# Twelve blocks scaled and shifted on ScalarE in place of VectorE, and modulation units placed earlier, in a two-block transformer kernel

## What is computed

```python
mod = silu(c) @ w_ada + b_ada                  # c: 2048; w_ada: 2048 x 12288
sh1, sc1, gt1, sh2, sc2, gt2 = split(mod, 6)
h = rms_norm(x, g_pre_mix) * (1.0 + sc1) + sh1
proj = h @ w_in                                # conv, attention, index and gate inputs
...
mixed = (g_conv * y_conv + g_attn * y_attn) @ w_o
x = x + gt1 * rms_norm(mixed, g_post_mix)
h = rms_norm(x, g_pre_ffn) * (1.0 + sc2) + sh2
f = (silu(h @ w_gate) * (h @ w_up)) @ w_down
x = x + gt2 * rms_norm(f, g_post_ffn)
```

## Time and profile before

| | us |
|---|---|
| median of 3 runs (2555.86 to 2557.14) | 2556.08 |
| the profiled execution | 2557.15 |
| its span, first to last instruction | 2555.3 |
| TensorE busy, matmuls | 2519.6 |
| VectorE busy | 1857.3 |
| ScalarE busy | 1269.6 |

### The profile page before, as it was taken

The page is one execution under the profiler, slowest core; times in us unless marked ns, Lnnn a source line. Parts: engine busy times, 40 slices in busy tenths (PEclk is TensorE's granted clock), DMA queues, the critical chain, the costliest instruction groups (busy, mean ns, idle before and its releaser), DMA issues.

```text
span 2555.3 us, 30126 instructions
## 1 busy us (share of the span) xinstructions
PE 2519.6 (99%) x11400; PEld 2072.9 (81%) x11400; DVE 1857.3 (73%) x2333; ACT 1269.6 (50%) x1733; POOL 3.9 (0%) x11
## 2 busy tenths in 40 slices
PE   7999999999999999999999999999999999999998
PEld 5888878888878888888888787888888888888886
DVE  7999999998877677556765667666666674456665
ACT  4445777764564444444444545554554444444443
POOL 0000000000000000000000000000000000000000
PEclk9999999999999999999999999999999999999999
DMA  9998666888946656665555555445555555555553
GB/s 378 355 355 318 216 214 217 294 296 313 361 168 229 231 210 238 243 231 210 217 215 198 185 194 180 162 170 197 181 193 188 196 208 198 189 195 198 187 194 130
DMA packets 80643, 578.23 MB, mean 226 GB/s; under 512 B 9022, under 2 KB 9318, under 8 KB 10737
## 3 DMA queue, kind: packets, MB, share of 16 engines
q1 hardware_dynamic: 78768, 566.92, 60.9%
q10 hardware_dynamic: 1218, 6.70, 0.7%
q0 software_dynamic: 512, 2.69, 0.3%
HBM read 574.15 MB, written 3.70 MB: 226 GB/s over the span
## 4 chain that ended last, share of the span: by engine, by line
PE 90%; DVE 5%; issue 1%; ACT 1%; DMA 0%; DVEq 0%; ACTq 0%; SPq 0%
PE bank L750 86%; DVE wlo L1643 2%; DVE raw L1653 1%; DVE cv L1854 1%; PE bank L689 1%; DMA raw<-in_w_in 0%; ACT whi L1075 0%; PE bank L905 0%; PE bank L953 0%; ACT PR L1075 0%; DVE PART L1716 0%; PE bank L867 0%; PE bank L996 0%; DVE SC L1798 0%; PE bank L1016 0%
## 5 line engine op out<-in xcount | busy, mean ns | idle before, releaser
L1643 DVE TENSOR_TENSOR wlo<-raw,whi 128x1024 fp32r<-128x1024 f32 x882 | 1072.9, 1223 | 632.8 <-ACT whi L1075 630.2
L1075 ACT ACTIVATE whi<-raw 128x1024 fp32r<-128x1024 f32 x882 | 929.5, 1058 | 1090.6 <-PE bank L750 942.6
L750 PE MATMUL bank<-whi,HTh 128*128 128x512 f32 x2560 | 697.7, 394 | 9.1 <-ACT HTh L1075 5.8
L750 PE MATMUL bank<-wlo,HTh 128*128 128x512 f32 x2560 | 687.0, 390 | 2.4 <-DVE wlo L1643 2.4
L750 PE MATMUL bank<-whi,HTl 128*128 128x512 f32 x2560 | 687.4, 390 | 0.0
L750 PEld LDWEIGHTS bank<-wlo,HTh 128*128 128x128 f32 x2560 | 480.9, 188 | 104.6 <-DVE wlo L1643 3.9
L750 PEld LDWEIGHTS bank<-whi,HTh 128*128 128x128 f32 x2560 | 473.9, 188 | 110.6 <-issue 10.8
L750 PEld LDWEIGHTS bank<-whi,HTl 128*128 128x128 f32 x2560 | 481.2, 188 | 101.4
L1653 DVE CUSTOM_DVE_ANT_0 raw<-raw,GT,VECS 128x2048 f32<-128x2048 f32 x96 | 224.8, 2346 | 0.4 <-DMA raw<-in_w_ada 0.2
L750 PE MATMUL bank<-whi,ACTl 128*128 128x512 f32 x704 | 188.8, 389 | 0.0
L750 PE MATMUL bank<-whi,ACTh 128*128 128x512 f32 x704 | 188.8, 389 | 0.0
(11 more groups left out here) (242 smaller groups left out, 1173.0 us busy)
## 6 DMA issues: line engine op xcount, KB each, us to landing
raw<-in_w_in SPq DMA_DIRECT2D x128, 1024.0 KB, 5.0
raw<-in_w_ada SPq DMA_DIRECT2D x96, 1024.0 KB, 6.1
raw<-in_w_gate SPq DMA_DIRECT2D x88, 1024.0 KB, 4.8
raw<-in_w_up SPq DMA_DIRECT2D x88, 1024.0 KB, 4.8
raw<-in_w_down SPq DMA_DIRECT2D x88, 1024.0 KB, 4.8
raw<-in_w_o SPq DMA_DIRECT2D x16, 1024.0 KB, 7.3
raw<-in_w_out SPq DMA_DIRECT2D x16, 1024.0 KB, 4.8
raw<-in_w_attn_out SPq DMA_DIRECT2D x8, 1024.0 KB, 5.0
```

Of the source, the lines that this page charges most:

```text
L750: i = e.matmul(bank[2 * ch.st + t][:, :], (xl if ps == 1 else xh)[:, k, tk(t)], (lo if ps == 2 else hi)[:, j * 512:j * 512 + 512], start=c ...
L1075: return e.activation(dst, src, ACT.Copy, scale=scale)
L1643: e.tensor_tensor(lo, src, r32(hi), S_).then_inc(lo_done, 1)
```

## The change

On VectorE, groups 2, 3 and 4 of `first_h` lose their scale-and-shift operations. ScalarE makes them, all of a group before its copies, as an activation with MA as scale and MB as bias, in place on xT, and waits for the group's MA first. VectorE's subtraction waits for both. In the plan, the condition for a modulation unit in the first stage becomes another one, and the share of the output projection 0.57 in place of 0.70.

```diff
--- before.py
+++ after.py
@@ -140,7 +140,7 @@
             else:
                 ch = p.chunk("part", (j, n), "h", "ACT" if j == 0 else "DVE", st=3 if n % 2 else 1)
             p.mm(ch, "w_in", (c * 4 + j) * 128 * 2048, 4, 512, 4 * j)
-            p.ada(early if j < 3 else p.later, int(n < (8 if j else 9)))
+            p.ada(early or p.later, int(n < (8, 8, 9, 10)[j] or (j, n) == (0, 8)))
     p.here("kiwi")
     p.ada(p.later, 1)
     p.mm(p.chunk("kiwi", 0, "h", "ACT", evictions=1), "w_kiwi", 0, 16, 80, 0)
@@ -165,7 +165,7 @@
         p.cols(p.chunk("conv", j, "ct", "DVE"), "w_conv_out", j, range(2), 2, 0.5)
     p.here("wo")
     for j in range(4):
-        p.cols(p.chunk("wo", j, "mix", "DVE", apart=j == 3), "w_o", j, range(4), 4, 0.7)
+        p.cols(p.chunk("wo", j, "mix", "DVE", apart=j == 3), "w_o", j, range(4), 4, 0.57)
     assert not p.later
     p.later += [(5, c) for c in range(16)]
     plan_ffn(p, 0, "")
@@ -417,7 +417,8 @@
     pro_pe = steps("pro_pe", list(R(4)))
     xt_pe = steps("xt_pe", list(R(0, 16, 2)))
     xt_act = steps("xt_act", list(R(0, 16, 2)))
-    fh_dve = steps("fh_dve", [(k, c) for cs_ in HG for k in ("h", "lo") for c in cs_])
+    fh_dve = steps("fh_dve", [(k, c) for cs_ in HG for k in (("h", "lo") if cs_[0] < 4 else ("lo",)) for c in cs_])
+    h_act = steps("h_act", list(R(4, 16)))
     fh_act = steps("fh_act", list(R(16)))
     rb_pe = steps("rb_pe", ["rows"])
     rb_act = steps("rb_act", ["rows"])
@@ -1198,8 +1199,15 @@
             yield 1
 
         def first_h(g):
+            if g > 1:
+                w.wait_ge(*first_mod(g))
+                w.wait_ge(*ada_of(0, HG[g][-1]))
+                for c in HG[g]:
+                    w.wait_ge(*xt_act(c // 2 * 2))
+                    e.activation(xT[:, c, :], xT[:, c, :], ACT.Identity, bias=MB[:, 0, c:c + 1],
+                                 scale=MA[:, 0, c:c + 1]).then_inc(*h_act.one(c))
             for c in HG[g]:
-                w.wait_ge(*fh_dve("h", c))
+                w.wait_ge(*(h_act(c) if g > 1 else fh_dve("h", c)))
                 copy(HTh[:, c, :], xT[:, c, :]).then_inc(*fh_act.one(c))
             yield 1
 
@@ -1675,13 +1683,13 @@
             stt(js, js, 1.0, vec("g1", HG[g][0], len(HG[g])), A_, M_).then_inc(*first_mod.one(g))
             w.wait_ge(*first_mod(g))
             w.wait_ge(*ada_of(0, HG[g][-1]))
-            for c in HG[g]:
+            for c in HG[g] if g < 2 else ():
                 w.wait_ge(*xt_act(c // 2 * 2))
                 e.tensor_scalar(xT[:, c, :], xT[:, c, :], MA[:, 0, c:c + 1], MB[:, 0, c:c + 1], M_, A_).then_inc(
                     *fh_dve.one("h", c))
             for c in HG[g]:
                 w.wait_ge(*fh_act(c))
-                w.wait_ge(*fh_dve("h", c))
+                w.wait_ge(*(fh_dve("h", c) if g < 2 else h_act(c)))
                 e.tensor_tensor(HTl[:, c, :], xT[:, c, :], r32(HTh[:, c, :]), S_).then_inc(*fh_dve.one("lo", c))
             yield 1
```

## The result

The changed kernel takes 2566.94 us (median of 5 runs, 2564.85 to 2568.35), the kernel before 2556.21 us beside it (5 runs, 2555.86 to 2557.14). The ratio is 1.0039 with a 95% interval of 1.0028 to 1.0050: **10.7 us slower**, between 7 and 13. Forecast were 6.0 us. The sign was right, the size was not, and the median lies 1.1 us above the range. The profiled execution took 2568.35 us with a span of 2566.5, so the two traces differ by 11.2 us.

A forecast was written before the change was run, and what follows sets the result against it. TensorE bounds the kernel generally, but VectorE is slower in the changed stage, by 0.30 us per 1 MB weight unit. 1.5 + 1.1 + 2.27 + 1.1 gives 6.0 us, so the median 2556.08 becomes 2562.1 us; range 2557.7 to 2565.8.

The forecast's parts named there:

- The three groups: Groups 2, 3, 4 of `first_h`: VectorE waits for ScalarE's scale-and-shift and gets 1.5, 1.1 and 1.1 us later.
- The unit at 58: Extra modulation unit at piece 58, where VectorE is the slower engine: costs 2.27 us.
- TensorE inherits it all: At the `qiT` copy near 214 us, TensorE takes over VectorE's whole delay, 6.0 us, whatever its cover before.
- Rival B: Delay partly hidden: ScalarE is quick and only the unit at piece 58 counts, 2.27 us, 2558.4; chance 0.14.
- rival C: Stalls at 202 and 218 us lower TensorE's granted clock: 2563.8 for one fall, 2565.5 for two; chance 0.12.
- the two units at 78 and 80: Extra modulation units before kiwi: 4.54 us more of VectorE, hidden by its waits and lead, so cost 0.
- the ring of four buffers moves on by one: Weight-load buffers: despite the extra units, each later load still waits for the same split of the same piece.
- The lead of VectorE's `lo`: At kiwi's first piece `lo` is ready 4.2 us before its pass; 3.85 us used, some 0.4 us to spare.
- The output projection: VectorE has three units less, 6.8 us, but TensorE doesn't wait for it there: gain 0.

The follow-up runs named there:

- the shift alone: Only the twelve scale-and-shift operations moved to ScalarE, with the old plan, against the kernel before: 2560.44 us, ratio 1.0014.
- a quarter of the volume: Only the units at 78 and 80 moved, their loads cut to 512 of 2048 values per row, products whole, against the kernel before: 2559.42 us.
- shorter products with it: Units at 78 and 80 moved, loads cut to a quarter and products to 256 of 2048 values, against the kernel before: 2558.78 us.
- the plan alone: Only the new places of the modulation units, scale-and-shift still on VectorE, against the kernel before: 2563.31 us, ratio 1.0024.
- the run with both cures: The changed kernel with VectorE's small MA instruction a slot earlier and ScalarE's transpose copies before its split: 2564.95 us, ratio 1.0031 to the kernel before.
- the units at 86 and 88: Two modulation units moved to pieces 86 and 88, behind kiwi, instead of 78 and 80, against the kernel before: 2559.58 us, ratio 1.0013.
- the early MA with the old plan: Twelve operations on ScalarE, VectorE's small MA instruction one slot earlier, plan as before, against the kernel before: 2557.06 us, ratio 1.0004.
- the unit at 58 alone: Only one modulation unit moved, to piece 58, with the old share of 0.70, against the kernel before: 2559.44 us, ratio 1.0008.
- the short products: Units at 78 and 80 moved, two products there over 256 of 2048 values, loads whole, against the kernel before: 2560.47 us, ratio 1.0015.

## Why the prediction was right, and where it failed

**The three groups: right.** 3.7 us forecast, 3.5 us alone on the chip (1.5 to 5.9). The durations taken from the convolution's rows (0.49 us apart) hold to a hundredth for four operations; groups 3 and 4 cost VectorE 1.3 us each, 0.2 more than forecast, in the hand-over, and group 2 1.5 for 1.5. That ScalarE's work turns into a wait was also shown by taking the wait away (+0.2 us).

**The unit at 58: right in the trace.** 2.27 forecast, 2.27 later in the changed kernel's trace between pieces 57 and 58, 2.5 alone, though with an interval that includes 0.

**That TensorE inherits it all: right here, but not by the chain alone that was named.** It is 5.9 us from piece 19 to 77 for 6.0, with stalls of 0.52 us at piece 20 (forecast 0.5), 1.57 at piece 60 (2), and 0.83 and 1.01 at the transposes (2.3 at `qiT`, met by two in place of one). Rival B is out. But "at 214 us TensorE takes over VectorE's whole delay, whatever cover it had before" was read from one execution. Among the seven kernels alike up to there, the load issued behind piece 63 took from 5.2 to 8.0 us to land, and TensorE's wait for `qiT` followed it:

| load landed in, us | 5.24, 5.29, 5.59 | 6.77 | 6.95 (before) | 7.22 | 7.95 |
|---|---|---|---|---|---|
| TensorE's wait for `qiT`, us | 0, 0, 0 | 0.5 | 0.63 | 1.0 | 2.0 |

So that wait of 0.63 us comes and goes. In the trace of the shift alone the load landed in 5.70 us, TensorE didn't wait, and its delay fell from 3.8 to 2.9 us.

**The clock at 202 and 218 us (rival C): did not happen.** (Its sums have a slip as well: with 1.5 us for each fall they are 7.5 and 9.0 us, 2563.6 and 2565.1.) The window from 200 to 220 us:

```profile
200.00:220.00 20.00, 17.60 (x77) 13.07 (x76) 18.11 (x21) 10.53 (x17) 0.00 (x0) 1.00 0.79 292
```

TensorE is idle for 2.4 of 20 us, and the granted clock stays at 1.00.

**The step that failed: "the two units at 78 and 80 ... I take 0".** They cost 2.8 us in the trace and 3.1 us alone. The lead of VectorE's `lo` was worked out correctly, and the `lo` was in time. But it was the wrong thing to watch. The prediction says that "the ring of four buffers moves on by one, so each later load still waits for the same split of the same piece". For the load that it had traced, and for the weights of pieces 64 to 76, that is so; for kiwi's it isn't, nor for those of pieces 60, 62, 78 and 82. With two more units in the ring, the buffer four back from kiwi is the new unit at 78, where it was the unit at 76. So the load goes out late, ScalarE's split waits, and TensorE is held at `qT`: the very chain that the prediction had traced at 214 us, and didn't look for a second time. The table above shows the step: the load goes out 5.7 us later than VectorE's delay alone would have it, against a lead of 1.6 us. How the cost divides isn't settled. By the medians, a quarter of the volume takes off 0.6 us (3.1 to 2.5) and shorter products with it another 0.6 (2.5 to 1.9), but shorter products with whole loads gave 3.7, and the intervals of these runs reach some 2 us to either side, so neither 0.6 can be told from nothing. Nor did the shorter products bring kiwi's data sooner, so a part of VectorE's time in it isn't ruled out.

**The output projection: no gain, as forecast, and 1.6 us off in the trace.** The waits there are the same within 0.2 us. The extra loss is the clock's stay at its lower level. Over the traces of the two kernels and all experiments, the kernel loses 1.6 to 1.7 us there where that stay is 10.2 us long (four traces), between -0.3 and 0.1 where it is 6.8 us, as before (six), and -0.7 to -0.3 where it is 3.4 us (seven). The plan doesn't sort them: 10.2 us stood with the shift alone, 3.4 us with the plan alone and its share of 0.57. But all four of the longest are among the eight traces with the operations on ScalarE, and of the changed kernel's five runs three had a mean granted clock of 0.996, which 9 of 115 runs of the kernel before had (a mean over the whole kernel, given to three places). So it isn't shown to be mere scatter, nor is a way shown in which the change could lengthen it; the shift alone has it in 2 of 11 runs.

The parts in the two traces add up: 0.9 ahead of group 2, 5.9, 2.8 and 1.6 us are 11.2. Of the 10.7 us between the medians, the parts alone account for 9.1. The changed kernel's two runs at 0.997, 2564.85 and 2565.84 us, are 9.1 us above before on average, so the remaining 1.5 us may well be this stay at the lower clock; two runs are few, in the kernel before the runs at 0.996 and 0.997 lie only 0.3 us apart on average, and it stays open. So do the 3 us of the run with both cures.

**A wait left unread.** The prediction's leave out TensorE's waits for `wlo`, 2.4 us in all, two of which, 0.36 and 1.27 us, lie at 320 and 325 us. No term of the sum rests on them, but it is there that the units at 86 and 88 then cost TensorE its time. VectorE's busy tenths, too, go down to four, not five.

**Not tried:** a fifth load buffer, which would loosen the ring. No version was measurably faster than the kernel before. The best of the changed ones, the early MA with the old plan, is equal to it, some 10 us faster than the change as made.

## What to carry to other kernels

Work moved from a full engine to a half-idle one only helps if the full engine has something else to do in its own order before it needs the result; put the instruction that feeds the helper a step earlier, or the work becomes a wait of the same length or more. An extra user of a ring of buffers changes what the next loads wait for: find, for each load behind it, which use now frees its buffer, and follow that load to the engine's queue behind it. When one such chain has been found in a stage (late load, split, copy behind it, TensorE), look for its every repetition before a cost is set to nothing.

## What was not expected of the hardware

Two things differ from one execution to another at one and the same place of the program. The first is how long TensorE's granted clock stays at its lower level: behind the output projection's end 3.4, 6.8 or 10.2 us, and near 41 us 3.4 us in fifteen traces and not at all in two (the unit at 58 alone, and the short products), though TensorE had been busy for only 1.31 and 1.24 of the 5 us from 36 to 41 us. Between the longest and the shortest stay at the output projection's end lie up to 2.4 us of time. The second is how long a load of 1 MB takes to land: 5.2 to 8.0 us for the same load in seven kernels alike up to there, and TensorE waited 0 to 2.0 us for it. Each is as large as the parts studied here, so a part of 2 us can be told in a single trace only where the same step is missing from every trace without its cause, as at kiwi.
